# First stage of a two-block transformer kernel: inputs scaled by the norm's weights only, each result multiplied by the norm's inverse on VectorE

## The reference

```python
def rms_norm(x, g):
    xf = x.astype(jnp.float32)
    y = xf * lax.rsqrt(jnp.mean(xf * xf, axis=-1, keepdims=True) + EPS)
    return (y * g.astype(jnp.float32)).astype(x.dtype)

def mixer_layer(u, w_in, ...):           # u = rms_norm(h, norm1_g)
    p = u @ w_in
    a, bv, bg, q, k, v, fg, gates = jnp.split(p, ...)
    ya = pool_mixer(a, ...) @ w_out_a
    yb = conv_module(bv, bg, ...) @ w_out_b     # bv * sigmoid(bg), 31-tap causal conv, layer_norm, silu
    logf = jax.nn.log_sigmoid(fg + b_forget)
    yc = forgetting_attention(heads(q), heads(k), heads(v), logf) @ w_out_c
    g = jax.nn.sigmoid(gates.reshape(B_, L, N_BRANCH, D))
    return (g[:, :, 0] * ya + g[:, :, 1] * yb + g[:, :, 2] * yc) @ w_o
```

## Time and profile before

| | us |
|---|---|
| median of 3 runs | 1912.21 (1911.74 to 1912.28) |
| the profiled execution | 1911.28 |
| its span, first to last instruction | 1909.6 |
| TensorE busy | 1890.5 |
| VectorE busy | 1391.0 |
| ScalarE busy | 957.6 |
| first real matmul starts | 10.47 |
| merge loop starts, about | 182 |

### The profile page before, as it was taken

The page is one execution under the profiler, slowest core; times in us unless marked ns, Lnnn a source line. Parts: engine busy times, 40 slices in busy tenths (PEclk is TensorE's granted clock), DMA queues, the critical chain, the costliest instruction groups (busy, mean ns, idle before and its releaser), DMA issues.

```text
span 1909.6 us, 26757 instructions
## 1 busy us (share of the span) xinstructions
PE 1890.5 (99%) x9040; PEld 1522.1 (80%) x9040; DVE 1391.0 (73%) x2201; ACT 957.6 (50%) x1351; POOL 120.1 (6%) x163
## 2 busy tenths in 40 slices
PE   9999999999999999999999999999999999999998
PEld 9987888877777788876678888888886788888887
DVE  7986444575999876788857888853397778888534
ACT  5667433456777633678754333333366543333222
POOL 0200000001000000045600000000101000000000
PEclk9999999999999999999999999999999999999999
DMA  5220333326999625510013333333341133333332
GB/s 196 87 70 12 92 95 99 99 85 218 358 355 351 220 61 166 138 49 3 3 47 100 99 93 94 99 100 110 100 126 35 57 99 99 92 95 99 100 110 88
DMA packets 68634, 219.39 MB, mean 115 GB/s; under 512 B 11648, under 2 KB 14880, under 8 KB 68416
## 3 DMA queue, kind: packets, MB, share of 16 engines
q1 hardware_dynamic: 64240, 212.46, 34.0%
q10 hardware_dynamic: 4304, 5.77, 1.2%
HBM read 209.05 MB, written 2.10 MB: 111 GB/s over the span
## 4 chain that ended last, share of the span: by engine, by line
PE 93%; DVE 5%; ACT 2%; issue 1%; DMA 0%; POOL 0%; DVEq 0%; ACTq 0%; SPq 0%; POOLq 0%
PE psum L1205 64%; PE psum L1729 7%; PE psum L1703 2%; PE psum L1931 2%; PE psum L1748 2%; PE psum L1640 1%; PE psum L1712 1%; PE psum L1377 1%; PE psum L1896 1%; PE psum L2118 1%; PE psum L1904 1%; PE psum L1783 1%; PE psum L1849 1%; DVE sig L3469 1%; DVE psum L4282 1%
## 5 line engine op out<-in xcount | busy, mean ns | idle before, releaser
L1205 PE MATMUL psum<-x_hi,w_hi 128*128 128x512 f32 (+1 forms) x1336 | 490.5, 378 | 0.0
L1205 PE MATMUL psum<-x_hi,w_lo 128*128 128x512 f32 (+1 forms) x1336 | 486.9, 375 | 0.0
L1205 PE MATMUL psum<-x_lo,w_hi 128*128 128x512 f32 (+1 forms) x1336 | 486.8, 375 | 0.0
L3179 DVE TENSOR_TENSOR w_lo<-raw,w_hi 128x1024 fp32r<-128x1024 f32 x243 | 296.3, 1221 | 187.1 <-ACT w_hi L2240 186.6
L2240 ACT ACTIVATE w_hi<-raw 128x1024 fp32r<-128x1024 f32 x243 | 256.0, 1055 | 188.0 <-DMA raw<-stream 187.3
L1205 PEld LDWEIGHTS psum<-x_hi,w_hi 128*128 128x128 f32 x1336 | 245.0, 188 | 46.4 <-issue 1.7
L1205 PEld LDWEIGHTS psum<-x_lo,w_hi 128*128 128x128 f32 x1336 | 245.0, 188 | 45.8 <-issue 1.2
L1205 PEld LDWEIGHTS psum<-x_hi,w_lo 128*128 128x128 f32 x1336 | 244.9, 188 | 45.5
L1205 PE MATMUL psum<-hid_hi,w_hi 128*128 128x512 f32 (+2 forms) x710 | 261.1, 375 | 0.5 <-DVE hid_lo L4397 0.5
L1205 PE MATMUL psum<-hid_lo,w_hi 128*128 128x512 f32 (+2 forms) x710 | 259.7, 373 | 0.0
L1205 PE MATMUL psum<-hid_hi,w_lo 128*128 128x512 f32 (+2 forms) x710 | 259.6, 373 | 0.0
(11 more groups left out here) (705 smaller groups left out, 2937.0 us busy)
## 6 DMA issues: line engine op xcount, KB each, us to landing
raw<-stream SPq DMA_DIRECT2D x251, 512.0 KB, 3.6
raw<-experts SPq DMA_DIRECT2D x70, 512.0 KB, 5.2
raw_more<-experts SPq DMA_DIRECT2D x68, 512.0 KB, 5.3
staged<-staged ACTq DMA_DIRECT2D x64, 64.0 KB, 2.9
out_fm<-resid SPq DMA_DIRECT2D x7, 256.0 KB, 2.2
resid<-x_fm SPq DMA_DIRECT2D x3, 528.0 KB, 7.2
consts<-consts_in SPq DMA_DIRECT2D x1, 1373.0 KB, 14.0
staged<-staged SPq DMA_DIRECT2D x20, 64.0 KB, 2.4
```

Source lines behind the costliest of these rows:

```text
L1205: last = pe.matmul(o, wt[:, slot, k * P:(k + 1) * P], m[part], start=start and p == 0, stop=stop and p == 2, skip_group_check=True)
L3179: dve.tensor_tensor(w_lo[:, slot, :], raw[:, slot, :], w_hi[:, slot, :].bitcast(F32), ALU.subtract)\
```

## The change

The fully normed input is gone. The input times the norm's weights is written once, into `XH` and `XL`, and all units of the stage use it. VectorE multiplies every result of the stage (entries, values, keys, queries and the merge's gates) by the inverse, kept in `INV1`, as it reads it from PSUM; ScalarE reads them no more, and the gates' sigmoid works on the staged result. The reading of the pooled results and the branches' products stays on ScalarE. bv0 and bv1 run one after the other, the norm's sum after both. `WARM` goes from 28 to 23. SyncE issues the first input tiles ahead of the second weight unit and holds later loads back until earlier ones have landed. The forget gate's bias moves from the read into the two instructions behind it. VectorE's hand-written order is new, and its convolution taps reach further into the attention. The second `glu` buffer moves, so ScalarE need not wait for the convolution in `keep_fox`.

```diff
-WARM = 28
+WARM = 23
...
-            for s in range(2):
-                sp.dma_start(raw[:, s, :], stream[s, :, :]).then_inc(raw_loaded[s], 16)
+            sp.dma_start(raw[:, 0, :], stream[0, :, :]).then_inc(raw_loaded[0], 16)
             sp.dma_start(H[:, 1, :], x_in[:, 1, :]).then_inc(x_loaded[1], 16)
-            for i in range(1, 4):
-                sp.dma_start(H[:, 2 * i:2 * i + 2, :], x_in[:, 2 * i:2 * i + 2, :]).then_inc(x_loaded[min(i + 1, 3)], 16)
+
+            sp.wait_ge(x_loaded[0], 32)
+            sp.dma_start(H[:, 2:4, :], x_in[:, 2:4, :]).then_inc(x_loaded[2], 16)
+
+            sp.wait_ge(raw_loaded[0], 16)
+            for i in range(2, 4):
+                sp.dma_start(H[:, 2 * i:2 * i + 2, :], x_in[:, 2 * i:2 * i + 2, :]).then_inc(x_loaded[3], 16)
+            sp.dma_start(raw[:, 1, :], stream[1, :, :]).then_inc(raw_loaded[1], 16)
+
+            sp.wait_ge(x_loaded[2], 16)
             sp.dma_start(consts[:, 0:2 * P], consts_in[:, 0:2 * P]).then_inc(ones_loaded, 16)
             sp.dma_start(vecs[:, C:], vecs_in[:, C:]).then_inc(vecs_loaded, 16)
-            for s in range(2, SLOTS):
-                sp.dma_start(raw[:, s, :], stream[s, :, :]).then_inc(raw_loaded[s], 16)
+            sp.dma_start(raw[:, 2, :], stream[2, :, :]).then_inc(raw_loaded[2], 16)
+
+            sp.wait_ge(raw_loaded[1], 16)
+            sp.dma_start(raw[:, 3, :], stream[3, :, :]).then_inc(raw_loaded[3], 16)
+
+            sp.wait_ge(raw_loaded[2], 16)
             sp.dma_start(inv[:, :, :], invcnt_in).then_inc(consts_loaded, 16)
...
-            two_units(U["bv"], r, T1, early_x, (x_ready, X0["early"]), first_sum)
-            for n in range(U["bg"], U["v1"]):
-                early = n < U["bg"] + 2
-                unit(n, n % SLOTS, r + n - U["bv"], (r + n - U["bv"]) % PAIRS, T1, early_x if early else x_of(T1),
-                     (x_ready, X0["n1"]) if n == U["bg"] + 2 else None)
+            for n in range(U["bv"], U["v1"]):
+                unit(n, n % SLOTS, r + n - U["bv"], (r + n - U["bv"]) % PAIRS, T1, x_of(T1), (x_ready, X0["n1"]) if n == U["bv"] else None)
+                if n == U["bv"] + 1:
+
+                    pe.wait_ge(ones_loaded, 16)
+                    gathered_sum("n1", T1)
...
+            def rooted(r, n, out_, rows=P):
+
+                dve.wait_ge(unit_used, n + 1)
+                dve.wait_ge(lin_free, r)
+                dve.tensor_tensor(halves(out_), pair(r)[0:rows, :, 0:HALF], halves(INV1[0:rows, :]), ALU.mult).then_inc(lin_free, 1)
...
+            def query_result(c):
+
+                r = (R["q1a"], R["q1b"], R["q1b"] + 1, R["q1c"])[c]
+                dve.wait_ge(unit_used, U["q1"] + c + 1)
+                dve.wait_ge(lin_free, r)
+                dve.wait_ge(fk_ready, c + 1)
+                dve.scalar_tensor_tensor(out=fox_staged(c, T2), in0=pair(r)[:, 0, :], scalar=SCALE, in1=INV1[:, META:T1], op0=ALU.mult, op1=ALU.mult)\
+                   .then_inc(lin_free, 1)
...
+            query_result(0)
+            taps(43, 45)
             fox_queries_low(0)
             low_weights(18)
-            taps(53, 55)
+            taps(45, 47)
             for f in range(2):
                 read_fox_max(0, f)
+            query_result(1)
+            taps(47, 49)
             fox_queries_low(1)
-            taps(55, 57)
+            low_weights(19)
             for f in range(2, 4):
                 read_fox_max(0, f)
-            low_weights(19)
+            query_result(2)
             for f in range(4, 6):
                 read_fox_max(0, f)
             fox_meta_max(0)
             fox_queries_low(2)
-            taps(57, 2 * KS)
             low_weights(20)
+            query_result(3)
             low_weights(21)
...
+                if p == 0:
+                    taps(49, 55)
                 if p == 1:
                     fox_queries_low(3)
+                    taps(55, 2 * KS)
...
                     for g in range(3):
+
+                        dve.wait_ge(unit_used, U["merge"] + i * 8 + 4 * m + g + 1)
+                        dve.wait_ge(lin_free, r + i * 12 + g)
+                        dve.wait_ge(ev_used, e + i * 12 + g - (EV_SLOTS - 1))
+                        dve.tensor_tensor(staged(e + g, T2), pair(r + g)[:, 0, :], INV1[:, META:T1], ALU.mult).then_inc(lin_free, 1)
                         low_weights(U["merge"] + 4 * m + g + AHEAD, i, 8)
```

More of the change, by code:

```diff
@@ L1231, in unit, with two_units @@
                     mm.then_inc(unit_used if ends else lin_done, 1)
-            def two_units(n, r, t, src, ready, late_sum=None):
+            def two_units(n, r, t, src, ready):
                 take_pair(r)
@@ L2464, in keep_v1 @@
                     fox_rows()
-            token_results(U["v1"], R["v1"], L0["v1"], 4, T1, 4, keep_v1)
+            for x, (c, turned_) in enumerate(turning_order(4)):
+                if turned_:
+                    alone(L0["v1"] + c)
+                    act.wait_ge(lin_free, R["v1"] + x)
+                    keep_v1(c, pair(R["v1"] + x))
+                else:
+                    by_unit(U["v1"] + c)
+                    high_weights(U["v1"] + c + AHEAD)
             for half in range(2):
@@ L2556, in keep_fox @@
                 act.wait_ge(fpv_done, N_F * p + (half + 1) * F_TILES)
-                if p == 0 and half == 0:
-                    act.wait_ge(convolved, 2)
                 own, other = head_rows(half), other_rows(half)
@@ L2614, in _ @@
                         by_unit(n + i * 8 + 4 * m + min(k, 3))
-                    stage((r + j) % PAIRS, e + i * 12 + j, (e + j) % EV_SLOTS, T2, ACT.Sigmoid if k < 3 else ACT.Copy)
+                    if 1 <= k <= 3:
+                        gate(j - 1)
+                    if k >= 3:
+                        stage((r + j) % PAIRS, e + i * 12 + j, (e + j) % EV_SLOTS, T2)
                     if k not in (3, 4):
@@ L3196, in reciprocal_root @@
                 then(dve.reciprocal(TS[:, 2, 0:t], TS[:, 2, 0:t]))
-            def normed(gain, count0, t, hi, lo, used, after={}):
-                if used:
-                    dve.wait_ge(unit_used, used)
-                for c in range(C + 1):
-                    if c < C:
-                        if count0 + c >= 2:
-                            dve.wait_ge(x_ready, count0 + c - 1)
-                        dve.scalar_tensor_tensor(out=TS[:, c % 2, 0:t], in0=H[:, c, T1 - t:T1], scalar=vec(gain, c), in1=TS[:, 2, 0:t],
-                                                 op0=ALU.mult, op1=ALU.mult).then_inc(y_ready, 1)
-                    if c:
-                        dve.wait_ge(hi_ready, count0 + c)
-                        dve.tensor_tensor(lo(c - 1), TS[:, (c - 1) % 2, 0:t], hi(c - 1).bitcast(F32), ALU.subtract).then_inc(x_ready, 1)
-                        if c - 1 in after:
-                            after[c - 1]()
             def last_sides():
@@ L3373, in _ @@
                 if c == 0:
-                    for n in range(2):
-                        low_weights(n)
-                if c > 2:
-                    first_sum(c - 1)
-            first_sum(C - 1)
+                    low_weights(0)
+            low_weights(1)
+            for c in range(2, C):
+                first_sum(c)
             low_weights(2)
             low_weights(3)
-            reciprocal_root(R["n1"], T1)
-            def rooted(c, out_):
-                dve.wait_ge(unit_used, U["bv"] + c + 1)
-                dve.tensor_tensor(halves(out_), pair(R["in1"] + c)[:, :, 0:HALF], halves(TS[:, 2, :]), ALU.mult).then_inc(lin_free, 1)
+            dve.wait_ge(lin_free, R["n1"] + 1)
@@ new lines, in _, with entry_result, value_result @@
+            then(dve.reciprocal(INV1[:, :], TS[:, 2, 0:T1]))
+            def rooted(r, n, out_, rows=P):
+                dve.wait_ge(unit_used, n + 1)
+                dve.wait_ge(lin_free, r)
+                dve.tensor_tensor(halves(out_), pair(r)[0:rows, :, 0:HALF], halves(INV1[0:rows, :]), ALU.mult).then_inc(lin_free, 1)
+            def entry_result(c, out_, rows=P):
+                rooted(R["in1"] + c, U["bv"] + c, out_, rows)
+            def value_result(c):
+                rooted(R["v1"] + turning_order(4).index((c, False)), U["v1"] + c, spare(4 + c, T1))
```

139 lines of the change are left out of this document (68 added, 71 removed).

## The result

The changed kernel takes **1920.66 us** (median of 6 runs, 1919.16 to 1923.21), the kernel before 1912.34 in the same comparison (1911.74 to 1913.31): a ratio of 1.0046, 95% interval 1.0035 to 1.0056, so 8.3 us slower. The forecast was 1913.4 with 1910.5 to 1916.0. The profiled execution took 1920.39 us, 9.1 more than that of before.

What follows compares the result with a forecast made beforehand. TensorE, busy 1890.5 of 1909.6 us, was taken to set the end. Terms -1.62 + 0.7 - 0.5 + 0.1 + 2.5 = +1.2 us gave 1913.4 us against the median, 8-in-10 range 1910.5 to 1916.

Steps and rivals of the forecast that it cites:

- Five empties, 1.62 us: At the start, 23 empty matmuls for 28, at 0.324 us each, let real work begin at 8.85: gain 1.62 us.
- The last input load at 10.6 us, wait 0.7: In the first units, the load lands between 9.9 and 11.3, half way 10.6; TensorE waits 0.7 us (0 to 1.4).
- Rival 2: At the start, the last input load lands no sooner than before, 12.66 at the latest; wait 2.8 us, 1915.5; chance 0.12.
- t + 4.8: Earliest start of the second unit, in us, with t the time the last input load lands; it is wanted at 14.7.
- The start as a whole: First units: a gain of 1.62 us from fewer empty matmuls against a wait of 0.7 for the last input load.
- The fourth value unit, -0.5: At the fourth value unit, VectorE, its taps ended, reads the result at once, removing most of TensorE's 0.64 us wait: gain 0.5.
- Norm and results, 0: Entries to queries: VectorE drops 11.8 us of norm work, gains 10.5 of PSUM products, all beside TensorE: cost 0 (to 3.6).
- Query units, +0.1: Between second and third maxima, VectorE's 6.7 us of work nearly fills TensorE's 6.85: loss 0.1 us (0 to 1).
- The attention, +2.5: Seven taps behind the third head pair's maxima (4.64 us) make TensorE's fourth fill of the next pair wait 2.5 us, once.
- rival 3: In the attention, TensorE's clock falls in the 2.5 us wait, costing up to 8.6 us more: 1922; chance 0.07.
- Merge loop, 0: In the merge loop, 24 products on half-busy VectorE replace ScalarE's reads: cost 0; without that cover 16.6 us.
- Everything behind it, 0: Behind the merge loop, in code the change does not touch: no term in the sum, gains only inside the first 210 us.

Runs made afterwards that it cites:

- e4: The changed kernel without SyncE's five waits between the first loads, their order kept: 1920.33 us, ratio 1.0024 to 1.0051.
- e6: The changed kernel with late taps split ten and three, 28 empty matmuls, no SyncE holds, fourth value product ahead of two taps: 1911.35 us.
- e1: The changed kernel with late convolution taps split ten and three behind the second and third head pairs' maxima, not six and seven: 1916.56 us.
- e8: The changed kernel with 28 empty matmuls and the late taps split eight and five: 1915.71 us, ratio 1.0005 to 1.0023.
- e2: The changed kernel with 28 empty matmuls in place of 23: 1918.40 us, ratio 1.0023 to 1.0050.
- e5: The changed kernel with the late taps split ten and three and 28 empty matmuls: 1914.09 us, ratio 1.0001 to 1.0019.
- e9: The changed kernel with taps split ten and three, 23 empty matmuls at the start and five more inside the first unit: 1913.38 us.
- e3: The kernel before with 23 empty matmuls in place of 28, nothing else: 1912.61 us, ratio 0.9994 to 1.0012.

## Why the prediction was wrong, point by point

- **What bounds the kernel: right.** TensorE's busy time is the same to 2 us, and every loss is a wait of TensorE or its clock.
- **Five empties, 1.62 us: the size was off.** 9.06 / 28 is a mean over two speeds. At the speed of the last ones five take 1.13.
- **The last input load at 10.6 us, wait 0.7: the step failed.** "The holds on SyncE cost nothing by this count" was wrong by 1.0 us, and the last packets came another 1.2 us behind the count of bytes. It was usable at 12.39; without holds at 11.78 (e4) and 10.73 (e6), and 10.6 had been the estimate. Rival 2 came about. By the prediction's own formula, t + 4.8 = 17.2 for the second unit against a start at 9.34, the wait is 2.0 us and not 2.8, since the real work also began later than I had it; 1.56 of it stood ahead of the fifth chunk. The start as a whole: -0.92 forecast, +0.5 measured.
- **The fourth value unit, -0.5: the step failed,** at "VectorE, which has ended its taps by then". It was in a tap for 0.43 us more. e6 gets 0.4 of it back by the order of two lines.
- **Norm and results, 0: right.** No wait for VectorE between 25 and 77 us.
- **Query units, +0.1: right in size.** The lag grows from 0.47 to 0.7 us (L1358, 129.7 against 130.4) and is back at 0.2 at 143 us.
- **The attention, +2.5: right in place, cause and size.** 2.52 us, once, at the fourth fill; e1 takes it away and e8 halves it by the 0.66 us a tap.
- **The clock, rival 3 with a chance of 0.07: this was the mis-sized chance.** The lag over the wait grows by 4.3 us, so the fall costs 1.8, not up to 8.6: the clock comes back after 3.4 us. "It decides as soon as the clock falls at all" was wrong too: 1913.4 + 1.8 = 1915.2 lies inside the range. Over all runs TensorE waited nine times for 1.9 to 2.5 us (the attention in after, e2 and e4; the loop in after, e1 and e4; the start in e1, e5 and e8), and the clock fell behind six of them (for 3.4 us five times, for 6.8 us in e4's attention); behind waits of up to 1.6 us it never did. "TensorE: Matmul & The Clock Gate", section "Why this matters for your kernels", of the Trainium skill, has it that TensorE falls back to the lower rate when it idles between bursts; the runs agree, with the addition that it is not every time.
- **Merge loop, 0: right.** From L1531 to L1868 both kernels need 619 us.
- **Everything behind it, 0: the step that failed and cost most, 3.9 us.** "It can gain only where TensorE begins its real work late or waits inside the first 210 us" was taken for the losses as well, so the sum had no term for code that the change does not touch, and no reason was given for leaving it out. The traces showed two instruction fetches on two small transfers there, 3.2 us of lag, and e9 moved the loop from 188.5 to 185.3 us by TensorE's instruction count alone.

1913.4 + 1.4 (start) + 0.5 (value unit) + 1.8 (clock) + 3.9 (loop) = 1921.0, against 1920.66. Without the loop it would be 1917.1, still over the range's 1916.0; without the start's miss too, inside it. The terms are those of one profiled execution.

## What to carry to other kernels

Lay out what each wait of the engine that sets the end may grow to, and where it comes near 2 us, count the clock on top: here moving ten and three taps in place of six and seven was worth 4.1 us. A load has landed when its last packet is through, here 1.2 us behind the count of bytes, and holding loads back cost bandwidth here (292 to 340 GB/s against 360 to 400). And before a small loss is put down to an edit, compare the lag of the two traces at many places: a loss in code that nobody touched may be an instruction fetch that fell on a small transfer, and five empty matmuls more or less moved it here.

## What was not expected of the hardware

- An instruction fetch (16 KB, 1.1 to 1.4 us in one packet) delayed the last two packets of a 2 KB transfer by 0.6 to 1.3 us in the 11 hits. In the kernel after ScalarE resumed 2.05 us later by it, TensorE idled 2.1 us. The packets explain 1.3 us of ScalarE's delay; the other 0.7 I have not settled. "DMA: Bandwidth & Descriptors", section "Queues, rings and completion order", of the Trainium skill says that a DMA engine takes its queues in turn and drains a whole packet before it changes; with the fetch as one packet of 1.39 us the trace agrees, as far as times alone can show it.
- Where the fetches fall depended on the number of TensorE's instructions ahead (e1 against e9), in jumps: 24, 25, 28 and 30 empties give the same place in that stage of the kernel before, 23 another.
- With 28 empties the loop of the changed kernel still takes about 1 us longer than before. VectorE and ScalarE have other instruction counts there too, and at 894.28 us VectorE's four small steps are followed by 0.24 us of idling beside an 8 KB fetch; this was not tested.
- The clock rose from 1.2 to 2.4 GHz (the empties' pace doubled) at 4.5 us in one execution (e3) and at 7.3 in another (after), with the same empties up to there, so what an empty costs differs from execution to execution.
